# Weight residues subtracted in two halves, and one squared-sum matmul moved two steps up

## The reference

```
first block:   h += [pool_mixer(p), sgu_mixer(u, v)] @ w_out     with p, u, v from rmsnorm(x) @ w_in
               h += cross_attention(rmsnorm(h), memory of 256 tokens)   (4 heads)
               h += conv_ffn(rmsnorm(h))          (width 2816, 3-tap causal convolution, silu gate)
               x  = rmsnorm(h)
second block:  q, k, v, a, b = split(rms_norm(x) @ w_in_2)
               attn = stick_breaking_attention(rms_norm(q), rms_norm(k), v)   (8 heads of 64)
               c    = silu(layer_norm(conv31(a * sigmoid(b))))
               x += [attn, c] @ w_out_2
               x += (silu(conv3(gate)) * val) @ w_down_2,  gate, val from rms_norm(x) @ w_up_2

stick-breaking: z = q k^T / 8;  weight[t,s] = exp(log_sigmoid(z[t,s]) + sum over s<j<t of log_sigmoid(-z[t,j]))
```

## Time and profile before

| | us |
|---|---|
| median of 3 runs | 1292.04 (1288.03 to 1292.2) |
| the profiled execution's own time | 1293.05 |
| span in its trace, first to last instruction | 1291.3 |
| PE busy (5590 matmuls) | 1258.5 |
| DVE, ACT, POOL busy | 609.3, 495.7, 527.5 |

### The profile page before, as it was taken

How to read it: one execution, slowest core, us unless ns; L and a number is a source line. 1 busy time by engine, 2 the same in 40 slices (tenths; PEclk the granted TensorE clock), 3 DMA queues, 4 the chain that set the end, 5 groups by cost and what they waited for, 6 DMA issues and landing times.

```text
span 1291.3 us, 16174 instructions
## 1 busy us (share of the span) xinstructions
PE 1258.5 (97%) x5590; PEld 1019.5 (79%) x5590; DVE 609.3 (47%) x882; ACT 495.7 (38%) x655; POOL 527.5 (41%) x244
## 2 busy tenths in 40 slices
PE   8889999999999999999999989899999999999999
PEld 6878888778888888888878766567888888888887
DVE  8893333343653155415564767675443313331332
ACT  6313452234443244314462244556533313332331
POOL 4654553223445344534454433000544453435343
PEclk9889999999999999999999999889999999999999
DMA  7333332112323222322232221000323232223222
GB/s 285 117 128 98 102 112 97 49 49 82 98 97 114 83 97 97 99 97 85 68 126 97 85 95 54 12 1 1 129 83 97 82 121 91 97 82 114 94 73 78
DMA packets 34033, 118.40 MB, mean 92 GB/s; under 512 B 4032, under 2 KB 4160, under 8 KB 33856
## 3 DMA queue, kind: packets, MB, share of 16 engines
q1 hardware_dynamic: 33696, 117.49, 27.4%
q10 hardware_dynamic: 288, 0.24, 0.1%
HBM read 115.61 MB, written 2.10 MB: 91 GB/s over the span
## 4 chain that ended last, share of the span: by engine, by line
PE 89%; DVE 6%; ACT 2%; issue 2%; DMA 1%; POOL 0%; SPq 0%; ACTq 0%; DVEq 0%; POOLq 0%
PE ps L1122 26%; PE ps L1124 26%; PE ps L1123 26%; PE ps L1429 2%; PE ps L1412 1%; PE ps L1287 1%; DVE slab L853 1%; PE ps L1309 1%; PE ps L1456 1%; ACT xg_hi L441 1%; DVE ps L736 1%; DMA h<-x_t 1%; PE ps L1179 1%; PE ps L1180 1%; PE ps L1181 1%
## 5 line engine op out<-in xcount | busy, mean ns | idle before, releaser
L339 POOL TENSOR_TENSOR w_lo<-w_raw,w_hi 128x1024 fp32r<-128x1024 f32 x215 | 517.2, 2409 | 736.3 <-ACT w_hi L425 373.8
L1122 PE MATMUL ps<-xg_hi,w_hi 128*128 128x512 f32 x960 | 380.1, 396 | 10.8 <-DVE slab L668 5.2
L1123 PE MATMUL ps<-xg_lo,w_hi 128*128 128x512 f32 x960 | 375.7, 391 | 0.0
L1124 PE MATMUL ps<-xg_hi,w_lo 128*128 128x512 f32 x960 | 375.6, 391 | 0.0
L1122 PE MATMUL ps<-y_hi,w_hi 128*128 128x512 f32 (+1 forms) x608 | 232.3, 382 | 0.0
L1124 PE MATMUL ps<-y_hi,w_lo 128*128 128x512 f32 (+1 forms) x608 | 230.6, 379 | 0.0
L1123 PE MATMUL ps<-y_lo,w_hi 128*128 128x512 f32 (+1 forms) x608 | 230.5, 379 | 0.0
L1122 PEld LDWEIGHTS ps<-xg_hi,w_hi 128*128 128x128 f32 x960 | 181.8, 189 | 50.8 <-issue 6.8
L1123 PEld LDWEIGHTS ps<-xg_lo,w_hi 128*128 128x128 f32 x960 | 181.8, 189 | 38.5 <-issue 1.4
L1124 PEld LDWEIGHTS ps<-xg_hi,w_lo 128*128 128x128 f32 x960 | 181.5, 189 | 38.2
L425 ACT ACTIVATE w_hi<-w_raw 128x1024 fp32r<-128x1024 f32 x124 | 130.4, 1052 | 126.4 <-PE ps L1124 126.4
(11 more groups left out here) (194 smaller groups left out, 1077.8 us busy)
## 6 DMA issues: line engine op xcount, KB each, us to landing
w_raw<-weights SPq DMA_DIRECT2D x199, 512.0 KB, 3.3
w_raw<-weights SPq DMA_DIRECT2D x16, 384.0 KB, 2.9
out_t<-h SPq DMA_DIRECT2D x8, 256.0 KB, 2.0
h<-x_t SPq DMA_DIRECT2D x3, 512.0 KB, 9.4
slab<-mem_t SPq DMA_DIRECT2D x2, 512.0 KB, 11.1
slab<-mats_in SPq DMA_DIRECT2D x1, 1024.0 KB, 5.3
w_raw<-weights SPq DMA_DIRECT2D x2, 256.0 KB, 3.9
h<-x_t SPq DMA_DIRECT2D x2, 256.0 KB, 4.8
```

The source lines that it names most:

```text
L339: nc.gpsimd.tensor_tensor(w_lo[:, s, :], w_raw[:, s, :], w_hi[:, s, :].bitcast(F32), ALU.subtract).then_inc(w_lo_ready, 1)
L1122: pe.matmul(out, w[0], x[0], start=first, stop=False)
L1123: pe.matmul(out, w[0], x[1], start=False, stop=False)
L1124: return pe.matmul(out, w[1], x[0], start=False, stop=last)
```

## The change

Two edits. First, POOL subtracts the residue of a block in two instructions of 128x512, and the first raises `w_lo_half`, the second `w_lo_ready`. PE waits for `w_lo_half` at the start of a block and for `w_lo_ready` ahead of its first k of 4 or more; for the token blocks it is one wait per k. `first_lo` of block 0 becomes `w_lo_half`. SP still waits for `w_lo_ready`. Second, `qk_sum(7)` stands ahead of `s_cumulate(0)` in PE's list, where it stood behind it.

```diff
-        w_hi_ready, w_lo_ready = sem("w_hi_ready"), sem("w_lo_ready")
+        w_hi_ready, w_lo_half, w_lo_ready = sem("w_hi_ready"), sem("w_lo_half"), sem("w_lo_ready")
...
             def weights_lo(b, s):
                 pool.wait_ge(w_hi_ready, b + 1)
-                nc.gpsimd.tensor_tensor(w_lo[:, s, :], w_raw[:, s, :], w_hi[:, s, :].bitcast(F32),
-                                        ALU.subtract).then_inc(w_lo_ready, 1)
+                for half, done in ((slice(0, BLK // 2), w_lo_half), (slice(BLK // 2, BLK), w_lo_ready)):
+                    nc.gpsimd.tensor_tensor(w_lo[:, s, half], w_raw[:, s, half], w_hi[:, s, half].bitcast(F32),
+                                            ALU.subtract).then_inc(done, 1)
...
             dve.wait_ge(first_hi, 1)
             nc.vector.tensor_tensor(w_lo[:, 0, 0:SEQ], w_raw[:, 0, 0:SEQ], w_hi[:, 0, 0:SEQ].bitcast(F32),
-                                    ALU.subtract).then_inc(first_lo, 1)
+                                    ALU.subtract).then_inc(w_lo_half, 1)
...
                 if begin:
-                    pe.wait_ge(w_lo_ready, b + 1)
+                    pe.wait_ge(w_lo_half, b + 1)
...
                 for n, k in enumerate(order):
+                    if k >= DT // 2 and (n == 0 or order[n - 1] < DT // 2):
+                        pe.wait_ge(w_lo_ready, b + 1)
...
                     k = 2 * part + kk
-                    if b == 0:
-                        pe.wait_ge((first_lo, w_lo_ready)[kk], 1)
-                    else:
-                        pe.wait_ge(w_lo_ready, b + 1)
+                    pe.wait_ge((w_lo_half, w_lo_ready)[kk], b + 1)
...
                 for s in range(4):
-                    pe.wait_ge(w_lo_ready, first + s + 1)
                     for kk in range(2):
+                        pe.wait_ge((w_lo_half, w_lo_ready)[kk], first + s + 1)
...
-                s_cumulate(hd)
                 if hd == 0:
                     qk_sum(7)
+                s_cumulate(hd)
```

More of the change, by code:

```diff
@@ L239, in build @@
         loaded_x = [sem(f"loaded_x{i}") for i in range(5)]
-        loaded_first, first_hi, first_lo, loaded_gains = sem("loaded_first"), sem("first_hi"), sem("first_lo"), sem("loaded_gains")
+        loaded_first, first_hi, loaded_gains = sem("loaded_first"), sem("first_hi"), sem("loaded_gains")
         loaded_cols, loaded_mats = sem("loaded_cols"), sem("loaded_mats")
         w_loaded = [sem(f"w_loaded{s}") for s in range(RING)]
-        w_hi_ready, w_lo_ready = sem("w_hi_ready"), sem("w_lo_ready")
+        w_hi_ready, w_lo_half, w_lo_ready = sem("w_hi_ready"), sem("w_lo_half"), sem("w_lo_ready")
         blocks_done, banks_freed = sem("blocks_done"), sem("banks_freed")
```

## The result

The changed kernel takes 1271.8 us (median of four runs, 1268.4 to 1274.7) against 1290.4 for the kernel before on the same chip: the ratio is 0.9856 (95%: 0.9824 to 0.9888). The forecast was 1283.4 with a range down to 1276. The sign was right and the size was not: 18.6 us, where the sum had 8.6. Runs of one kernel lie up to 11 us apart (31 runs of the kernel before on one chip: 1283.0 to 1293.8), so small differences between kernels are to be read with their intervals.

What follows compares the result with a forecast made beforehand. PE was taken to bound the kernel, with 89% of the chain that ended last. From the profiled 1293.05 us, 5.05 (attention) and 3.5 (front) off gave 1284.5; that execution being 1.0 above the median, 1283.4, range 1276 to 1288.5.

Steps and rivals of the forecast that it cites:

- The direct effect of the half semaphore: At block starts: no PE wait for `w_lo` ends last, so an earlier first half gains 0.
- The added wait: PE's one more wait per block: between 0 and 0.19 us, taken as 0 from the even matmul pace over waits.
- Rival (d): Whole kernel slower: mid-block wait leaves weight loads bare, 0.19 us for some 200 blocks, 38 us, so 1322; chance 4%.
- The second edit: Attention: `qk_sum(7)` starts earlier, so ACT's `s_weights(0)` and PE's scores of head 2 come 5.05 us earlier.
- may be gained on top: Attention, behind the stall: 3.2 us from PE at half clock, left out of the sum, possible if shorter idling keeps the clock up.
- The front: Start to block 16: halved POOL instructions shorten DVE's waits, so the fifth and sixth keys and block 16 come 3.5 us earlier.
- To the second copy: Front, 10.9 to 48 us: halves end DVE's first copy 4.6 us earlier, the next gains 1.0, so DVE is 5.6 ahead.
- From the second copy to the keys: Front, 51.2 to 88.8 us: POOL and DVE take turns without a gap; halves add 3.1 us, pushed-back residues return about 1.0.
- POOL's fixed cost: Front, crowded stretch: 0.28 us more per halved residue, times 11 gives 3.1 us more.
- all of PE's earlier gains end in this wait: Ahead of block 16: PE's wait for DVE's memory keys stays, so only the keys' 3.5 us counts.
- rival (a): Front gains 8 us because DVE gets the ports first each time: 1279, or 1276 with the 3.2 of clock; chance 20%.
- 1.0 above the median: Whole kernel: the profiled execution of 1293.05 us lies 1.0 above the median of runs, lowering the forecast to 1283.4.

Runs made afterwards that it cites:

- the last kernel: Changed kernel with idle matmuls in PE's idle times (start, gate block, wait for `conv_moved`, attention); 1265.6 us, ratio 0.9822 to the kernel before.
- move only: Kernel before with only `qk_sum(7)` put ahead of `s_cumulate(0)`, residues whole; 1281.8 us against 1290.9, ratio 0.9926.
- added wait: Kernel before with only PE's additional wait in mid-block, on the whole residue's semaphore, always fulfilled; 1290.8 us against 1290.9, ratio 1.0008.
- filler in attention: Kernel before with 24 idle matmuls where PE waits ahead of the scores of head 2; 1286.5 us, ratio 0.9977.
- halves 1 to 8: Kernel before with POOL's residues in halves for blocks 1 to 8 only, one semaphore; 1284.8 us against 1290.7, ratio 0.9956.
- halves 9 to 19: Kernel before with POOL's residues in halves for blocks 9 to 19 only, one semaphore; 1286.3 us, ratio 0.9971.
- 17 to 19 held: Kernel before, residues whole, POOL holding those of blocks 17 to 19 until DVE's fifth and sixth memory keys are out; 1287.4 us against 1292.3, ratio 0.9975.
- halves only: Kernel before with only the first edit: residues in two halves with a semaphore each, `qk_sum(7)` in its old place; 1278.9 us, ratio 0.9901.
- halves, one semaphore: Kernel before with residues in halves, only the second raising a semaphore, PE's waits and `qk_sum(7)` as before; 1281.5 us, ratio 0.9926.
- quarters: Changed kernel with each half residue cut once more for blocks 1 to 19, still two semaphores; 1268.5 us, ratio 0.9821 to the kernel before.

## Why the prediction was right and wrong

**The direct effect of the half semaphore: zero, and it is next to that.** With it and without it the changed kernel takes 1270.6 and 1272.3, in ranges that overlap. In the profiled executions the fronts are 128.01 and 128.22, and up to the gate block ahead of the second mixer another 0.2 is lost without it (523.98 and 524.18), 0.4 us in all.

**The added wait: zero, and it is.** 1.0008, with the last feed-forward at 381.99 us before and after. Rival (d) is out.

**The second edit: 5.05 us of stall, and it is.** PE's wait was to be 1.6 and is 1.5; ACT's chain of root, logs and weights moved as a whole (5.11 us from root to weights before and after), and the running sums didn't become the later wait. What the forecast left out as something that "may be gained on top" came as well: the attention is shorter by 6.6 us with the move alone, and by 9.3 and 7.7 in the two executions of after. The rest, 1.6 to 4.3, goes with the clock: 17.1 us of the attention were at half clock before, 10.2 with the move alone, 6.8 and 10.2 after. At the same 6.8 us of half clock the attention takes 102.77 with the stall (its idle time filled) and 96.75 after, so the move by itself is 6.0 in that pair. Before has two stretches at 0.50 there, of 10.2 us from 815.0 and of 6.8 from 845.7. The first execution of after has one, of 6.8:

```profile
797.80:804.60 6.80, 6.80 (x17) 4.25 (x17) 5.93 (x9) 4.44 (x4) 0.00 (x0) 0.50 0.00 0
804.70:860.00 55.30, 54.23 (x256) 34.36 (x255) 44.40 (x74) 33.29 (x37) 0.00 (x0) 1.00 0.00 1
```

The price of 3.2 us for the stretch fits what was found: with the stall kept and its idle time filled, the attention took 3.3 less. The choice to leave it out of the sum was the error of this part. (The idle time ahead of the scores of head 2 began at 810.5 by the earlier trace rows, not at 809.9; nothing hangs on it.) That the wait of 1.07 us had been followed by half clock was taken as a reason to leave the stretch in; half clock did follow the 1.5 us of after, but for a shorter time: 6.8 us in one execution, 6.8 and 3.4 in the other. It isn't all gain, either: the query and key stretch has 13.7 us at half clock after and 10.2 before, and takes 1.3 more. The stretch came out at 132.9 to 133.1 with whole residues and at 134.1 to 134.5 in the kernels with halves, except that with the first edit alone (132.91) and the last kernel, with its idle matmuls there (128.35). All those at 134.1 and more had 13.7 us at half clock in it, and all those at 133.1 and less 10.2. Why the clock falls for longer there with halves stays open. Each edit alone was without this loss, which is part of why their gains, 9.1 and 12.0, come to more than the 18.6 and 19.9 of both.

**The front: 3.5 expected, some 11 to 14 found.** This is the term that put the forecast out of its range. DVE's chain in the front, from the traces of eleven kernels (us; "residues" are those that POOL began between the end of DVE's second copy and the end of its fifth and sixth keys, with their time in that stretch; "held" is the number of DVE's steps there that took over 0.1 us longer than the shortest of their kind in any of these traces, and by how much all were longer):

| kernel | first copy ends | second copy | 5th, 6th keys | second copy to keys | residues, us | held, us | block 16 |
|---|---|---|---|---|---|---|---|
| before | 41.2 | 48.1 | 89.6 | 41.5 | 11, 28.4 | 11, 21.3 | 89.8 |
| move only | 40.2 | 44.9 | 86.2 | 41.3 | 11, 27.1 | 10, 21.2 | 86.4 |
| added wait | 40.0 | 47.0 | 86.3 | 39.3 | 11, 27.1 | 10, 19.1 | 86.4 |
| filler in attention | 41.2 | 48.1 | 87.5 | 39.5 | 11, 27.1 | 10, 19.3 | 87.7 |
| halves 1 to 8 | 35.3 | 41.2 | 82.8 | 41.6 | 11, 28.2 | 11, 21.4 | 82.9 |
| halves 9 to 19 | 40.1 | 47.0 | 83.7 | 36.7 | 10 in halves, 30.4 | 17, 16.5 | 83.8 |
| 17 to 19 held | 40.9 | 47.8 | 83.0 | 35.2 | 8, 22.4 | 8, 15.0 | 84.1 |
| halves only | 34.4 | 40.2 | 78.9 | 38.7 | 10½ in halves, 31.5 | 19, 18.5 | 79.1 |
| halves, one semaphore | 34.5 | 40.8 | 75.8 | 35.0 | 9 in halves, 26.3 | 15, 14.8 | 77.6 |
| after | 34.7 | 39.4 | 75.0 | 35.6 | 10 in halves, 28.6 | 16, 15.5 | 75.5 |
| quarters | 33.6 | 38.3 | 68.0 | 29.7 | 7½ in quarters, 28.2 | 20, 9.6 | 75.5 |

*To the second copy.* The forecast had the first copy end at 36.6 and DVE 5.6 us ahead at the second, at 42.5. With halves they end at 34.4 to 35.3 and 39.4 to 41.2; the step was right, and its size short by one to three us. Two of its rows: DVE's residues of x, of which the earlier trace rows had a mean of 1466 ns, and the second copy, which took 0.29 unhindered in after, and in kernels with whole residues at that place 2.54 (halves 9 to 19, 17 to 19 held) or 0.29 (move only).

```profile
L694 DVE SCALAR_TENSOR_TENSOR xg_lo<-h,cols,xg_hi 128x512 fp32r<-128x512 f32 x6 | 7.1, 1184 | 0.8 <-ACT xg_hi L442 0.8
...
39.09 0.29 DVE L711 COPY wide<-rcol 128x256 f32<-128x256 f32 x1 [0.81 <-POOL rcol L355]
```

The halves of blocks 1 to 8 alone carry this lead through to block 16: 82.9 against 86.4 to 89.8, and 6.0 us in the medians.

*From the second copy to the keys.* This is the step that failed: "The two engines simply take turns, without a gap, and cutting one party's turns in two saves nothing; it adds POOL's fixed cost". The forecast had the stretch longer by 3.1 and shorter by 1.0. With whole residues it is 39.3 to 41.6 us long, with halves 35.0 to 36.7 in three kernels and 38.7 in the fourth, so 4 to 5 us shorter as a rule. What the traces show in its place stands in the column "held". DVE has the same 48 steps in this stretch in every kernel, and without the waiting they take 20.1 to 20.2 us in all eleven traces; the rest is DVE waiting. With whole residues 10 or 11 steps wait, 1.9 to 2.1 us each; with halves 15 to 19 wait, but for 0.95 to 0.98 us each; with quarters 20 wait, for 0.47. So the wait of one step falls with the size of POOL's instruction, and the number of steps that have to wait grows by less than that. The four parts of the error:

1. "Without a gap" was misread. The earlier trace rows has POOL busy for 29.3 of 37.6 us, so idle for 8.3; from the second copy to the keys it was idle for 12.2 of 41.5 us, and for 5.4 of 35.6 after. The two weren't simply taking turns: DVE was held in 11 of its 48 steps and ran the others beside POOL or while POOL was idle.
2. POOL's fixed cost was taken too high, from a power of two columns. Two halves in a row take 2.54 to 2.59 us and a whole one 2.39 to 2.41, so it is 0.15 to 0.2 a block, and 1.7 to 2.2 for eleven blocks, not 3.1.
3. Residues are pushed back more than by the 1.0 counted. With halves 9 to 10½ residues lie in the stretch and not 11. They are the ones of blocks that PE releases late, and PE doesn't need them yet. That fewer residues shorten the stretch by themselves is shown by the kernel that holds residues 17 to 19: with whole residues, eight of them in the stretch, and 8 steps held for 1.9 us each, it is 35.2 long, as with halves.
4. Where DVE and POOL do alternate, a turn costs less than its parts. A whole residue and a DVE step of 0.70 add up to 3.09 us, a half and such a step to 1.99; the starts of POOL's instructions lie 2.87 to 2.88 and 1.70 to 1.72 apart. So the sum fails after as well: DVE's steps of the held kind are 11.5 us unhindered and 20 halves at 1.29 are 25.8, together 37.3, more than the 35.6 of the stretch; with 30 quarters at 0.73 it is 33.4 against 29.7.

Two lines of DVE before, from 51.2 to 88.8, then three after, from 42.4 to 75.0, and the window of that stretch:

```profile
L886 DVE TENSOR_SCALAR slab<-slab,bna,tiny 128x512 f32<-128x512 f32 x4 | 4.1, 1071 | 0.0
...
L861 DVE SCALAR_TENSOR_TENSOR slab<-slab 128x512 f32<-128x512 f32 x3 | 2.1, 692 | 0.1
```
```profile
L887 DVE TENSOR_SCALAR slab<-slab,bna,tiny 128x512 f32<-128x512 f32 x4 | 5.9, 1532 | 0.0
L862 DVE SCALAR_TENSOR_TENSOR slab<-slab 128x512 f32<-128x512 f32 x3 | 5.2, 1739 | 0.1
...
L859 DVE TENSOR_TENSOR slab<-slab,corr 128x16 f32<-128x16 f32 x3 | 3.6, 1199 | 0.1
```
```profile
42.40:75.00 32.60, 32.60 (x211) 29.82 (x210) 32.02 (x38) 9.01 (x9) 27.77 (x20) 1.00 0.42 146
```

The small step of the earlier trace rows takes 1.20 us and not 2.26, as foreseen. The steps of line 861 (862 after), of which none was held before, were all held after: this is how the number of held steps grows. How the hardware chooses between the two in detail, no run here resolves. "SBUF — State Buffer" of the Trainium skill, Who interferes with whom, gives an exclusive lock for a whole instruction. The halved wait of the small step agrees with it; the distance of 1.71 for a half and a step of 0.70 says that a stretch can't be costed by adding up both engines' times under that rule. It is also why "meet only in semaphores", in the section on the chip, is too narrow: DVE waits here for POOL without one.

What misled me was a sum. The 26.3 of POOL and 11.5 of DVE added up to 37.8, the stretch of 37.6 us itself, and I read that as proof of strict turns. From the second copy on the same work took 39.3 to 41.6 in the executions with whole residues, and in three of the kernels with halves 35.0 to 36.7: it was one number that happened to fit.

*Behind the keys.* That "all of PE's earlier gains end in this wait" holds while it exists: the forecast kept it, at 86.3. It went, and its price with it twice: once as the wait, once as the half clock behind it, which the sum left out, 2.4 us (50.6 for 53.0).

So rival (a), "The front gains much more", is nearest to what happened, which was more still: it had 8 us for the front and 8.2 for the attention with the clock. Measured were 7.7 to 9.3 for the attention, 1.3 to 1.5 back in the query and key stretch, and for the front 11 to 14 (126.1 and 128.0 in two executions of after, 138.6 to 140.0 in three of whole residues; the 142.8 of the profiled execution of before would make it up to 17). Its ground, that DVE gets the ports first each time, isn't what the traces show: DVE still waited 15.5 us for them after.

**The profiled execution of before.** It was taken as typical, 1.0 above the median. In its front it was not: whole residues gave fronts of 138.6 (move only), 138.7 (added wait), 138.8 (idle matmuls ahead of block 16) and 140.0 (ahead of the scores) in other executions, and 142.8 in this one. In the table, DVE's chain differs by 3.2 us at the second copy (44.9 to 48.1) and by 2.2 in the stretch to the keys (39.3 to 41.5) between executions whose lists are the same so far: the second copy was held in three of them (2.5 us) and not in the fourth (0.29), so which engine comes first isn't fixed. A forecast for the front from this one trace carries an error of up to 4 us for that alone, and the range had nothing for it.

## What to carry to other kernels

Where GpSimd holds up VectorE on the way to a wait of the bound engine, count VectorE's held steps and the wait of each: here a halved GpSimd instruction halved the wait of a step and raised the number of held ones by less, and GpSimd's work that wasn't needed yet fell behind VectorE's chain. A part of the same was had with whole instructions by holding that work back. A wait of TensorE can have a second price, the half clock behind it, and belongs into the sum with its row as soon as the wait is to go. And where two engines contend, one execution's trace is one draw: a sum that fits one stretch should be tried on a second one before it becomes the mechanism.

## What the runs showed of the hardware beyond that

**The clock at the start differs between executions of one kernel.** These are the windows from 6.6 to 9.6 us (first matmuls of block 0), of the repeated execution of after and of the first one:

```profile
6.60:9.60 3.00, 2.96 (x7) 2.41 (x8) 2.56 (x4) 3.00 (x5) 0.00 (x0) 1.00 1.01 408
```
```profile
6.60:9.60 3.00, 2.81 (x12) 2.36 (x13) 2.47 (x5) 3.00 (x5) 0.00 (x0) 1.00 1.02 412
```

The same kernel does 7 matmuls in one and 12 in the other, 0.43 and 0.23 us apart. The column of the granted clock shows 1.00 for both, but the record of the clock begins at 11.0 us in the one and at 5.9 in the other; by the pace, which is that of half clock, the repeated one ran at 1.2 GHz until then. It costs 1.9 us: block 1 starts at 14.24 and 12.33, and the fronts are 128.01 and 126.11. The difference is there on one chip too: the kernels with idle matmuls ahead of block 16 and ahead of the scores of head 2 (in the kernel before) ran on one chip, have the same list up to there, and make 13 and 7 matmuls in this window. This was the whole of what I had first put down to the half semaphore.

**Idle matmuls in a wait can keep the clock up.** 24 of them in the stall of 5.8 us left the wait as it is, and the attention took 3.3 us less; 10 in the attention of after brought it from 96.75 and 98.39 to 94.43, with no stretch at half clock left in it. With the same 10 in the last kernel 6.8 us at half clock stayed. They cost when they are too many: ahead of block 16 they ended 1.6 us behind what PE was waiting for.
